# Gate and up layers of the feed-forwards: one 512-column matmul for both activation parts, summed on VectorE

## The reference

```python
def swiglu(x, wg, wu, wd):
    return (jax.nn.silu(x @ wg) * (x @ wu)) @ wd

# first block, one layer
hid = jax.nn.relu(rmsnorm(h, norm_mlp[l]) @ w_ff1[l])
h = h + (hid * hid) @ w_ff2[l]
return rmsnorm(h, norm_final)

# second block, two layers
for l in range(DEPTH_2):
    x = layer_norm(ALPHA * x + 0.5 * swiglu(x, ffn1_wg[l], ffn1_wu[l], ffn1_wd[l]), ...)
    mix = token_mixer(x, w_in[l], ...)
    x = layer_norm(ALPHA * x + mix, ...)
    x = layer_norm(ALPHA * x + 0.5 * swiglu(x, ffn2_wg[l], ffn2_wu[l], ffn2_wd[l]), ...)
```

## Time and profile before

| | us |
|---|---|
| median of 3 runs | 1756.4 (1756.06 to 1756.79) |
| span of the profiled execution | 1756.8 |
| TensorE busy | 1703.3 (97%) |
| VectorE busy | 1050.3 (60%) |
| ScalarE busy | 770.8 (44%) |
| GpSimd busy | 66.3 (4%) |

### The profile page before, as it was taken

The page is one execution under the profiler, slowest core; times in us unless marked ns, Lnnn a source line. Parts: engine busy times, 40 slices in busy tenths (PEclk is TensorE's granted clock), DMA queues, the critical chain, the costliest instruction groups (busy, mean ns, idle before and its releaser), DMA issues.

```text
span 1756.8 us, 31591 instructions
## 1 busy us (share of the span) xinstructions
PE 1703.3 (97%) x13326; PEld 1607.1 (91%) x13326; DVE 1050.3 (60%) x1381; ACT 770.8 (44%) x990; POOL 66.3 (4%) x84
## 2 busy tenths in 40 slices
PE   6999899999999999999999999999999999999998
PEld 6877699999999999887899999999999877999998
DVE  5967565555644557775665455654567765664445
ACT  5456544333433335655443343433346554344233
POOL 1331000000000000000000000000000000000000
PEclk9998999999999999999999999999999999999999
DMA  6512243565456554522435655455464522535551
GB/s 198 168 48 73 96 145 108 180 191 177 173 189 192 169 178 122 180 73 73 145 107 181 191 173 184 146 167 191 145 183 127 168 73 73 169 120 183 177 170 68
DMA packets 213877, 257.87 MB, mean 147 GB/s; under 512 B 13866, under 2 KB 188324, under 8 KB 213796
## 3 DMA queue, kind: packets, MB, share of 16 engines
q1 hardware_dynamic: 213604, 256.68, 46.1%
q10 hardware_dynamic: 192, 0.04, 0.0%
HBM read 255.65 MB, written 1.05 MB: 146 GB/s over the span
## 4 chain that ended last, share of the span: by engine, by line
PE 92%; DVE 4%; SPq 1%; ACT 1%; issue 1%; POOL 0%; DMA 0%; POOLq 0%; DVEq 0%; ACTq 0%
PE bank L429 77%; PE bank L1442 2%; PE bank L570 2%; PE bank L1469 2%; PE bank L1029 1%; PE bank L577 1%; DVE wl L397 1%; PE bank L1455 1%; PE bank L1018 1%; PE bank L1470 1%; PE bank L1475 1%; PE bank L1445 0%; POOL stat L584 0%; PE bank L1019 0%; SPq L786 0%
## 5 line engine op out<-in xcount | busy, mean ns | idle before, releaser
L429 PE MATMUL bank<-uh,wh 128*128 128x256 f32 (+1 forms) x2528 | 726.8, 287 | 12.3 <-ACT tmp L1256 3.5
L429 PE MATMUL bank<-ul,wh 128*128 128x256 f32 (+1 forms) x2528 | 717.2, 284 | 0.0
L429 PE MATMUL bank<-uh,wl 128*128 128x256 f32 (+1 forms) x2528 | 717.1, 284 | 0.0
L397 DVE TENSOR_TENSOR wl<-raw,wh 128x2048 fp32r<-128x2048 f32 (+3 forms) x235 | 523.4, 2244 | 274.7 <-ACT wh L390 273.6
L390 ACT CAST wh<-raw 128x2048 fp32r<-128x2048 f32 (+3 forms) x235 | 431.8, 1859 | 190.3 <-PE bank L429 184.3
L429 PEld LDWEIGHTS bank<-uh,wh 128*128 128x128 f32 (+1 forms) x2528 | 484.6, 192 | 17.6 <-issue 7.3
L429 PEld LDWEIGHTS bank<-ul,wh 128*128 128x128 f32 (+1 forms) x2528 | 484.8, 192 | 1.0 <-issue 1.0
L429 PEld LDWEIGHTS bank<-uh,wl 128*128 128x128 f32 (+1 forms) x2528 | 484.6, 192 | 0.0
L429 PE MATMUL bank<-hh,wh 128*128 128x256 f32 (+1 forms) x928 | 264.2, 285 | 2.1 <-DVE hl L554 2.1
L429 PE MATMUL bank<-hh,wl 128*128 128x256 f32 (+1 forms) x928 | 263.3, 284 | 0.0
L429 PE MATMUL bank<-hl,wh 128*128 128x256 f32 (+1 forms) x928 | 263.2, 284 | 0.0
(11 more groups left out here) (320 smaller groups left out, 1716.0 us busy)
## 6 DMA issues: line engine op xcount, KB each, us to landing
raw<-ffn_wg SPq DMA_DIRECT2D x44, 1024.0 KB, 6.0
raw<-ffn_wu SPq DMA_DIRECT2D x44, 1024.0 KB, 5.4
raw<-ffn_wd SPq DMA_DIRECT2D x44, 1024.0 KB, 5.1
raw<-w_ff SPq DMA_DIRECT2D x32, 1024.0 KB, 5.3
raw<-w_in SPq DMA_DIRECT2D x28, 1024.0 KB, 5.3
raw<-w_out SPq DMA_DIRECT2D x12, 1024.0 KB, 5.0
raw<-w_gate SPq DMA_DIRECT2D x8, 1024.0 KB, 5.3
raw<-w_in SPq DMA_DIRECT2D x16, 512.0 KB, 5.5
```

The lines of the kernel that those rows point to most:

```text
L397: ins = dve.tensor_tensor(dst, src, upper.bitcast(F32), ALU.subtract)
L429: mm = pe.matmul(o, w, x, start=start and n == 0, stop=stop and n == 2, skip_group_check=True)
```

## The change

The two parts of the activations, `uh` and `ul`, are now the two halves of one buffer `u_parts`. In gate and up layers the upper weights meet both parts in one matmul of 512 columns that fills a whole bank: the left half holds the products with the upper part, the right half those with the lower part. A second matmul of 256 columns adds the lower weights times the upper part to the left half. So 128 features take a bank: gate uses banks 4 and 5, up uses 6 and 7. VectorE adds the two halves with a tensor_reduce over pairs, into `gates` (which is free during the feed-forwards). Silu reads that sum instead of bank 4. In the first block Relu and square are one VectorE instruction (max with 0, times itself) in place of ScalarE's Relu and VectorE's product. TensorE's next gate slab waits for the reduce (`gate_sum`) and no more for the activation. Other layers use `mm3` as before.

```diff
-        bank = [ctx.enter_context(nc.psum_tensor(f"bank{i}", [P, 512], F32)) for i in range(8)]
+        banks = ctx.enter_context(nc.psum_tensor("bank", [P, 8, 512], F32))
+        bank = [banks[:, i, :] for i in range(8)]
...
-        uh = sb("uh", [P, KD, T], F32R)
-        ul = sb("ul", [P, KD, T], F32R)
+        u_parts = sb("u_parts", [P, 2, KD, T], F32R)
+        uh, ul = u_parts[:, 0], u_parts[:, 1]
...
-                    mm = mm3(pe, bank[b][:, f * T:(f + 1) * T],
-                             slab_view(wh, slot, KD, WCOLS)[:, k, f * P:(f + 1) * P],
-                             slab_view(wl, slot, KD, WCOLS)[:, k, f * P:(f + 1) * P],
-                             uh[:, k, :], ul[:, k, :], k == 0 and (f == 0 or ready is None), k == KD - 1)
+                    pe.matmul(two(bank[b + f]), slab_view(wh, slot, KD, WCOLS)[:, k, f * P:(f + 1) * P], u_parts[:, :, k, :],
+                              start=k == 0, stop=False, skip_group_check=True)
+                    mm = pe.matmul(bank[b + f][:, 0:T], slab_view(wl, slot, KD, WCOLS)[:, k, f * P:(f + 1) * P], uh[:, k, :],
+                                   start=False, stop=k == KD - 1, skip_group_check=True)
                 mm.then_inc(used[slot], 1)
 
             def gate(n, more=0, i=None, ready=None):
                 if i is not None:
-                    pe.wait_ge(ffn_act, i + ih0)
+                    pe.wait_ge(gate_sum, i + ih0)
                 up_half(n, more, 4, ready)
...
+        gate_z, up_z = gates[:, 0:2, :], gates[:, 2:4, :]
+
+        def halves(b):
+            return banks[:, b:b + 2, :].rearrange("p f (h t) -> p f t h", h=2)
+
         def ffn_act_engine(act, n0, iters, has_up, ih0):
             def epilogue(what, n, i, more):
-                if what != "gate":
-                    return
-                slot, u = slabs[n][2:]
-                if not (isinstance(i, int) and i == 0):
-                    act.wait_ge(hid_ready, i + ih0)
-                act.wait_ge(used[slot], more + u + 1)
-                act.activation(act_out[:, :, :], two(bank[4]), ACT.Silu if has_up else ACT.Relu).then_inc(ffn_act, 1)
+                if what == "gate" and has_up:
+                    if not (isinstance(i, int) and i == 0):
+                        act.wait_ge(hid_ready, i + ih0)
+                    act.wait_ge(gate_sum, i + ih0 + 1)
+                    act.activation(act_out[:, :, :], gate_z, ACT.Silu).then_inc(ffn_act, 1)
             ffn_split(act, act_round, n0, iters, has_up, epilogue)
 
         def ffn_dve_engine(dve, n0, iters, has_up, ih0):
             def epilogue(what, n, i, more):
 
-                if (has_up and what != "up") or (not has_up and what == "gate" and not (isinstance(i, int) and i == 0)):
+                if what == "gate":
+                    slot, u = slabs[n][2:]
+                    dve.wait_ge(used[slot], more + u + 1)
+                    if has_up and not (isinstance(i, int) and i == 0):
+                        dve.wait_ge(ffn_act, i + (ih0 - SLABS1))
+                    dve.tensor_reduce(gate_z, halves(4), AX.X, ALU.add).then_inc(gate_sum, 1)
+                    if has_up or not (isinstance(i, int) and i == 0):
+                        return
+                if has_up and what == "down":
                     return
...
-                slot, u = slabs[n][2:]
-                dve.wait_ge(used[slot], more + u + 1)
-                dve.wait_ge(ffn_act, i + ih0 + 1)
-                other = two(bank[5]) if has_up else act_out[:, :, :]
-                dve.tensor_tensor(hid[:, :, :], act_out[:, :, :], other, ALU.mult).then_inc(hid_step, 1)
+                if has_up:
+                    slot, u = slabs[n][2:]
+                    dve.wait_ge(used[slot], more + u + 1)
+                    dve.tensor_reduce(up_z, halves(6), AX.X, ALU.add).then_inc(up_sum, 1)
+                    dve.wait_ge(up_sum, i + (ih0 - SLABS1 + 1))
+                    dve.wait_ge(ffn_act, i + (ih0 - SLABS1 + 1))
+                    dve.tensor_tensor(hid[:, :, :], act_out[:, :, :], up_z, ALU.mult).then_inc(hid_step, 1)
+                else:
+                    if what == "down":
+                        slot, u = slabs[n][2:]
+                        dve.wait_ge(used[slot], more + u + 1)
+                    dve.wait_ge(gate_sum, i + ih0 + 1)
+                    dve.scalar_tensor_tensor(out=hid[:, :, :], in0=gate_z, scalar=0.0, in1=gate_z,
+                                             op0=ALU.max, op1=ALU.mult).then_inc(hid_step, 1)
```

More of the change, by code:

```diff
@@ L276, in hybrid_ssm_attention_kernel @@
         ffn_act = sem("ffn_act")
+        gate_sum, up_sum = sem("gate_sum"), sem("up_sum")
         hid_ready = sem("hid_ready")
@@ L477, in ffn_pe @@
             if has_up:
-                up_half(n0 + 1, 0, 5)
+                up_half(n0 + 1, 0, 6)
             n1 = n0 + (2 if has_up else 1)
@@ L483, in ffn_pe @@
                 if has_up:
-                    up_half(n1 + 2, i - 1, 5)
+                    up_half(n1 + 2, i - 1, 6)
             n1 += per * (iters - 2)
@@ L487, in ffn_pe, with ffn_split @@
             if has_up:
-                up_half(n1 + 1, 0, 5)
+                up_half(n1 + 1, 0, 6)
             down(n1 + per - 1, iters - 2)
             down(n1 + per, iters - 1, last=True)
-        def ffn_split(eng, do, n0, iters, has_up, epilogue, leave_last=False):
+        def ffn_split(eng, do, n0, iters, has_up, epilogue, leave_last=False, then=None):
             per = 3 if has_up else 2
@@ L501, in step @@
                     do(eng, n + 2, more)
+                if then is not None:
+                    then(what, i)
             def turn(i, more, at):
```

## The result

The changed kernel takes 1776.72 us (median of 4, 1776.18 to 1777.52) where the kernel before took 1756.23 us beside it (4 runs). The ratio is 1.0113, 95% interval 1.01 to 1.0125: 1.1% slower. The forecast was 1776.0. The profiled execution has a span of 1775.8 us, 19.0 more than that of before.

What follows compares the result with a forecast made beforehand. TensorE was taken to set the time. From a span of 1756.8 us, +22.0 (second block) and -2.4 (first block) gave 1776.4, and 1776.0 us as the median; range 1759 to 1791, core 1768 to 1783 at 0.55.

Steps and rivals of the forecast that it cites:

- What bounds: TensorE sets the time; splits in the second block's turn have 0.71 us of room (up slab) and 1.24 us (down).
- The pair of matmuls: In gate and up slabs, one 512-column plus one 256-column matmul takes 350 ns, saving 0.16 us per slab.
- Rival 1: The weight load is what costs; a pair nears 320 ns, total 1755.6 or 1751.5 us; chance 0.09.
- rival 2: Half the surplus goes: the pair takes 333 ns, 0.43 us saved a slab, total 1762 us; chance 0.13.
- The reduce: VectorE's new sum of two PSUM halves for every gate and up slab takes 1.21 us, between 1.16 and 1.37.
- rival 4: The reduce is slower than the rows say, 1.37 us, giving a stall of 0.79 us and 1789.4 us; chance 0.13.
- Chain from gate to up: Second block: Silu, round and split wait for the reduce; 1.34 us added, a 0.63 us stall in 44 places.
- 0.15 us of waking: A TensorE that waits for a split starts its matmul 0.15 us after the split's end.
- Chain from up to down: Second block: 1.245 us added against 1.24 of room, so ten gate slabs a stage stay at 5.76 us.
- First block: 15 gate slabs gain 0.16 us each, -2.4 us in all; the first gate slab is put at nothing.
- Loads and multiply: Multiply takes 0.69 us from PSUM and SBUF alike; down-slab weights have 2.0 us of room.
- Rival 3: No gain from 512 columns: the pair takes 360 ns, total 1784 us; chance 0.10 (1783 to 1787).

Runs made afterwards that it cites:

- e1: The changed kernel with ScalarE rounding the up slab ahead of Silu in the second block; 1747.36 us, ratio 0.9945 to the kernel before.
- e5: The changed kernel with a second, unused reduce of the gate banks ahead of the real one, in the second block alone; 1830.8 us, ratio 1.042.
- e3: The kernel before, without the change, with both reorderings of e2; 1757.21 us, ratio 1.0001.
- e8: The kernel of e2 with the lower weights' matmul on 64 instead of 128 weight columns in gate and up slabs; 1738.5 us, one run.
- e6: The changed kernel with only VectorE's reordering of e2; 1777.93 us, ratio 1.012.
- e4: The changed kernel with the 512-column matmul cut into two of 256 on the same halves; 1788.63 us, ratio 1.0175.
- e2: As e1, and VectorE splits the down slab ahead of the up slab's epilogue, except in the last turn; 1746.54 us, ratio 0.9946.
- e7: The changed kernel without the lower weights' matmul in gate and up slabs; 1695.06 us, one run.

## Why the prediction was right, point by point

**What bounds: right.** The room of 0.71 us, read from one turn, is the number that decided: e1 and e5 bear it out, and e3 shows that as long as it is there the order is worth nothing.

**The pair of matmuls: right within 3 ns.** Taken at 350 ns. Measured 353 ns in the second block (5.65 / 16; in two turns gate and up slab together are 0.16 us shorter), 347 and 353 in turns in the first. The bound of 320 ns was not reached. Nor was the estimate of 325 ns by the rule of the Trainium skill, "TensorE: Matmul & The Clock Gate", "Back-to-back issue gap"; the page gives that rule for what it calls "the *isolated* single-MM gap", and each matmul here has a weight load ahead of it. Rival 1 and rival 2 fall with it: even with 5.55 us a slab (e8) a pair stays at 347.

**The reduce: right.** 1.21 taken, 1.22 measured. 1.37 and rival 4 are out.

**Chain from gate to up: right in size.** Forecast stall 0.63 us, with the whole 0.15 us of waking ahead of the first matmul. Measured in the first of the four feed-forwards: the down phase is 0.51 us longer than its matmuls, and the up slab (5.75) 0.10 longer than its own (5.65), together 0.61 us; e1 gives back 0.57 a turn. The waking is there, but split in two, as the start of that up slab shows:

```profile
527.23 0.50 PE L453 MATMUL bank<-u_parts,wh 128*128 128x512 f32 x1 [0.31 <-DVE wl L399]
527.56 0.28 PE L455 MATMUL bank<-u_parts,wl 128*128 128x256 f32 x1
527.68 0.39 PE L453 MATMUL bank<-u_parts,wh 128*128 128x512 f32 x1
527.91 0.28 PE L455 MATMUL bank<-u_parts,wl 128*128 128x256 f32 x1
```

The first matmul starts 0.06 us after the split and takes 0.33 us to the next; the second of its kind takes 0.23. In the three later feed-forwards VectorE starts the reduce 0.29 us after the gate slab, as forecast, and not 0.20:

```profile
1171.95 0.34 PE L431 MATMUL bank<-hh,wh 128*128 128x256 f32 x1
```

```profile
1172.24 1.22 DVE L550 TENSOR_REDUCE gates<-bank 128x512 f32<-128x1024 f32 x1 [0.40 <-PE bank L455]
```

There the down phase is 6.35 us and the stall 0.69. That is the 4.5 against 5.3 to 5.8 us in the table.

**Chain from up to down: the step that was wrong, with a small effect.** The forecast let this chain hold the gate slab at 5.76 us. Measured 5.65, the matmuls' own time, and e6 shows that the chain costs the changed kernel nothing. In the turn shown the split was over at 538.52, 5.54 us after the gate slab's start, not 5.61, and the down slab's matmul came 0.11 us behind it, not 0.15. So ten gate slabs a stage gained 0.11 us that I had given up: 4.4 us less. Against it stand the pair at 353 instead of 350 in 36 up slabs (1.8 us more) and a stall of 0.69 instead of 0.63 in three of the stages (2.0 us more). With the measured sizes the forecast's own sum gives 11 x 0.69 - 19 x 0.11 = 5.5 us for a later stage and 11 x 0.61 - 19 x 0.11 = 4.6 for the first: the table again.

**First block: right for the 15 gate slabs, not for the first one.** 15 x 0.155 = 2.3 us from 5.56 and 5.65, forecast 2.4. With the 1.5 us of the clock's place that would be -3.8, and the stretch has -3.4: the very first gate slab, which waits for the normalisation part by part and which the forecast put at nothing, takes 7.21 us where it took 6.69. Its cause stays open. In the second block the first gate slabs take 0.03 to 0.11 us less.

**Loads and multiply: right.** The multiply takes 0.69 us; TensorE's longest waits after name no load of a slab.

**Rival 3 (no gain from 512)** would be e4, which measured 1788.6 where I worked out 1784: out for the changed kernel. About 2 of the 4.6 us are the stall at 0.69 instead of 0.63.

The theory was put to the test by e1, e3, e4 and e5 and held, with e1 at 1747.4 for 1750 expected. Of e2 and e6 I expected up to 4 us and found none in the medians, and 1.3 in the starts of e2.

**How close it came is partly luck.** The mechanism and its size hold, but 1776.0 against 1776.7 needs the gate slabs' 4.4 us too few to stand against the 3.8 us of pair and stall, and the clock's -1.5 in the first block against its +1.55 behind the second feed-forward.

## What to carry to other kernels

When TensorE is the bound, look at every chain that must end before its next piece of work, and measure how much room each has: here 0.71 us. A step of 1.2 us on an engine that is 60% busy cost 0.6 us each time, since it stood ahead of Silu, and Silu ahead of a round that had nothing to do with it. Where an epilogue gets longer, first issue what the next slab needs and then the epilogue: that turned a change of +1.1% into -0.55% here, and e3 found it worth nothing where there was room.

## What the runs showed of the hardware

- A matmul of this type costs its columns at 2.4 GHz plus some 13 ns with 128 weight columns, at 256 columns (120.0) and at 512 (226 in e7; the four steps of the earlier trace rows have 230). Merging two matmuls saves one such surplus at best; in pairs with a 256-column one it saved 7 to 13 ns of 360.
- The same pairs run at one of two steady paces, 353 or 347 ns (slabs of 5.65 or 5.56 us); the faster is what the two matmuls cost apart, 226 + 120. In the first block they alternate from turn to turn. What chooses between them was not found.
- The list of waits understates what a wait costs. It has 0.31 us for the wait above (16.2 us in 40), where e1 gives back 0.57 a turn and 29 us in all; in the turn shown the missing 0.26 us is this: the matmul ahead of the wait has a record of 0.28 us though the next could start 0.12 us after it, and the second matmul after the wait is 0.10 us late.
